# Moving an expert loop within its instruction blocks, clearing sums earlier, and splitting the first picks

## The chip, the cores and the metric

The kernel runs on one core of a Trainium2 chip. The metric is the time of one execution on the device in microseconds; three executions of the kernel before gave 1177.3, 1177.52 and 1179.76, median 1177.52.

## The reference

The kernel computes three transformer layers on 256 tokens of width 1024, in fp32. The third (with its own normalisations, a recurrence, neighbourhood attention and gates) isn't touched here. Each of the first two ends in a mixture of experts:

```
g_prob = softmax(x @ w_group + b_group);  g_w, g_idx = top_k(g_prob, 1)     # one of 4 groups
e_logits = (x @ w_router + b_router)[g_idx]                                 # 4 experts in it
e_val, e_idx = top_k(e_logits, 2);  e_w = softmax(e_val)
gates = sum(one_hot(4 * g_idx + e_idx, 16) * g_w * e_w)
for e in range(16):
    hid = silu(x @ w_gate[e]) * (x @ w_up[e])
    y = y + gates[:, e] * (hid @ w_down[e])
```

Each token thus uses 2 of 16 experts, and all weights of all 16 are read: 6 MB per expert.

## The kernel before, in words

**Weights.** All large weights come through a ring of six slots of 2 MB in SBUF. SP issues one transfer per slot (L437 in the expert layers, L417 elsewhere), in the order of use, as soon as PE has reported that it is done with the slot's previous content (`unit_done`).

**Routing.** PE computes router logits; VectorE picks group and experts and writes a mask of tokens by experts. PE turns the mask into ranks by five small matmuls (L790 to L794): the rank of each token within its expert. VectorE makes of them a key per token and expert (L2203), and of the key the "picks" of a pair of experts: for 128 columns, which token stands in which (L2223 and L2226). Beside this, PE has the two gate rows (L593), copied out by ScalarE (L1437), and the matmuls of a group of the next modulation vector (`group_main`, L550) to do.

**The loop.** 16 experts go as 8 pairs, in a loop on each engine. For each pair PE multiplies the gathered tokens (128 columns in four chunks of 32) by the gate and up weights of the two experts, gathers the next pair's tokens (L826), turns `hid` (L908), scatters the previous pair's results by adding them to four banks of sums (L891), turns the weighted picks (L916), and multiplies by the down weights. The four banks of sums are cleared before the loop by four bf16 matmuls of zeros (`clear_sums`, L811). How many of the four chunks go to the first expert of the pair depends on the tokens: 2 is the usual split, 1 and 3 are uneven. Each of the three has its own copy of the code, so that there are three bodies for gate and up (64 matmuls of the program each, L870) and three for down (32 each), chosen by branches (`by_split`, L853 and L857). With "usual first" the usual body stands ahead of the others, and leaves by a branch over them; with "usual last" it stands behind them, and is entered by a branch. `ahead` and `later` are hints that tell the sequencer of a branch to come. A token that finds no place in its expert's columns goes through code for left-over tokens, which stands behind the loop and is branched over when there is none (L971).

**Where the code lies.** `pe.addr_align(256, 101, 0)` (L787) asks that the next instruction be loaded at slot 101 of a block of 256 instructions; the loader branches over what it leaves empty. It stands right ahead of the mask matmuls, in each of the two layers, so all bodies of the loop lie at fixed slots of their blocks.

**Order.** The order on each engine is written out by hand, as the code is; nothing is scheduled. Semaphores order the engines against each other.

Of the kernel before, what the change touches and what calls it, by code (L numbers as in the profile page):

```python
# [21 lines left out]
ALU = mybir.AluOpType  # L22
# [110 lines left out]
def program(nc, a, out):  # L133
    ctx = ExitStack()
    with ctx:
# [151 lines left out]
        def copied_at(group):  # L287

            return group + 1
# [171 lines left out]
        def _(pe):  # L461
# [93 lines left out]
            def group_whole(group, last):  # L555

                pe.wait_ge(sem("ada_ready"), 4 * group)
                pe.wait_ge(sem("modulation_summed"), summed_at(unit_of[f"ada{last}"]))
                part = sum_of(last)
                for g in range(4):  # L560
                    mm = pe.matmul(group_bank(group)[32 * g:32 * g + 32, :], ones[:, 0:32],
                                   part[:, 512 * g:512 * g + 512], start=True, stop=True, tile_position=(0, 32 * g))
                mm.then_inc(sem(f"group_{group}_whole"), 1)
# [200 lines left out]
            def experts(layer):  # L764
# [11 lines left out]
                mm.then_inc(sem("logit_parts_full"), 1)  # L776
                gate_row(gate, 0)
                pe.wait_ge(sem("constants_ready"), 2 * layer + 2)
                pe.wait_ge(sem("logit_parts_taken"), layer + 1)
                for t in range(TT):  # L780
                    mm = pe.matmul(ps[4][:, S + 20 * t:S + 20 * t + 20], logit_parts[:, t * P:(t + 1) * P], sel,
                                   start=True, stop=True)
                mm.then_inc(sem("logits_full"), 1)
                gate_row(gate, 1)
                group_main(group, (2,))

                pe.addr_align(256, 101, 0)  # L787
                pe.wait_ge(sem("mask_ready"), 2 * layer + 2)
                mask = rt[:, 512:512 + 32].rearrange("p (t e) -> p t e", e=EXPERTS)
                pe.matmul(ps[4][:, 384:400], lt, mask[:, 0, :], start=True, stop=True)  # L790
                pe.matmul(ps[4][:, 400:416], ones, mask[:, 0, :], start=True, stop=False)
                pe.matmul(ps[4][:, 400:416], lt, mask[:, 1, :], start=False, stop=True)
                pe.matmul(ps[4][:, 416:432], ones, mask[:, 0, :], start=True, stop=False)
                pe.matmul(ps[4][:, 416:432], ones, mask[:, 1, :], start=False, stop=True)\  # L794
                  .then_inc(sem("rank_full"), 1)
                group_main(group, (3,))

                def left_over():

                    pe.wait_ge(sem("ada_part_taken"), copied_at(group))  # L800
                    pe.wait_ge(sem("over_ready"), layer + 1)
# [3 lines left out]
                def clear_sums():  # L805

                    taken(pe, gate)
                    pe.wait_ge(sem("constants_ready"), 2 * layer + 3)
                    zero = hidT[:, 0:2, :].rearrange("p a b -> p (a b)").bitcast(BF16)
                    for b in range(4):  # L810
                        mm = pe.matmul(ps[b][:, :], zero[:, 0:P], zero, start=True, stop=True, skip_group_check=True)  # L811

# [126 lines left out]
                clear_sums()  # L939
# [4 lines left out]
                with pe.Fori(0, PAIRS) as j:  # L944

                    which = pe.snap(split_reg)
                    pe.reg_alu(uneven_reg, split_reg, 1, ALU.bitwise_and)
                    ahead = pe.mark_branch_hint_location(uneven_reg)
                    later = []
                    by_split("gate_up", which, lambda n: gate_up(j, n), "usual first", ahead)  # L950
                    with pe.If(j > 0):
                        results(j - 1)
                    with pe.If(j < PAIRS - 1):
                        gather(j + 1)
                    turn_hid(j)
                    with pe.If(j > 0):
                        scatter(j - 1)
                    turn_weights(j)
                    by_split("down", which, lambda n: down(j, n), "usual last", first_uneven=later[0])
                    pe.wait_ge(sem("g_cur_ready"), j + (done + 1))  # L960
# [278 lines left out]
        def _(act):  # L1239
# [109 lines left out]
            def group_copy(group):  # L1349
                if group in SUMMED_GROUPS:  # L1350
                    act.wait_ge(sem(f"group_{group}_whole"), 1)
# [382 lines left out]
        def _(dve):  # L1734
# [345 lines left out]
            def route(layer):  # L2080

                lg = rt[:, 0:40].rearrange("p (t c) -> p t c", c=20)
                dve.wait_ge(sem("logit_parts_full"), layer + 1)
                dve.tensor_copy(logit_parts, ps[4][:, 0:S]).then_inc(sem("logit_parts_taken"), 1)
                dve.wait_ge(sem("logits_full"), layer + 1)
# [50 lines left out]
                for t in range(TT):  # L2136
# [3 lines left out]
                       .then_inc(sem("mask_ready"), 1)  # L2140
# [34 lines left out]
                dve.wait_ge(sem("rank_full"), layer + 1)  # L2175
# [25 lines left out]
                dve.tensor_tensor(by_tile(over), by_tile(rank), slots_bc, ALU.is_gt).then_inc(sem("over_ready"), 1)  # L2201
# [3 lines left out]
                dve.wait_ge(sem("over_ready"), layer + 1)  # L2205
                return weights

            def experts(layer):
# [12 lines left out]
                def picks(j):  # L2221
# [5 lines left out]
                       .then_inc(sem("pick_ready"), 1)  # L2227

# [42 lines left out]
                picks(0)  # L2271
# [611 lines left out]
```

## Time and profile before

| | us |
|---|---|
| three executions | 1177.3, 1177.52, 1179.76 |
| the profiled execution | 1178.81 |
| its span | 1177.1 |
| PE busy | 1114.5 (95%) |
| VectorE busy | 414.2 (35%) |
| ScalarE busy | 272.4 (23%) |

PE is busy nearly all the time. The two expert loops run from 183.6 to 410 and from 576.3 to 810 us. Rows marked PE are matmuls, PEld weight loads; an fp32 matmul of the program shows as two of each. A timeline row merges neighbouring instructions of one kind: start, length, engine, line, count (x), and in brackets how long the engine had been idle and what ended that. "issue" means that the profile shows nothing the engine waited for. q1 is the queue that carries the weights, q8 the one with PE's instructions.

### The profile page before, as it was taken

The page shows a single profiled execution, that of the slowest core. Times are in us where ns is not written, and L with a number is a line of the kernel's source. Part 1 is how long each engine was busy: PE and PEld are TensorE (multiplying, and loading weights), DVE is VectorE, ACT ScalarE, POOL GpSimd, SP SyncE. Part 2 cuts the span into 40 slices and gives each one's busy share as a digit, 9 for nine tenths or more (in the row PEclk, how much of TensorE's full clock was granted, in tenths as well). Part 3 has the DMA queues.
Part 4 walks back from the last instruction along what each step waited for, and adds up shares of the span by engine and source line. Part 5 has one row for each costly group of instructions (what it writes and reads, how often), then busy time and mean ns, then how long its engine had stood idle before and what let it go on. Part 6 is the DMA issues. An engine that isn't in the chain of part 4 may idle for free.

```text
span 1177.1 us, 17038 instructions
## 1 busy us (share of the span) xinstructions
PE 1114.5 (95%) x6890; PEld 646.3 (55%) x6891; DVE 414.2 (35%) x1065; ACT 272.4 (23%) x579; POOL 91.5 (8%) x156
## 2 busy tenths in 40 slices
PE   3999989999999999989899999998999999999997
PEld 0756434444444378554344444444886878767883
DVE  0275254112111089943511111114541444341213
ACT  2214332111111031162211111114002555541201
POOL 0300030000000000230000000000010323210000
PEclk9999999999999999999899999998999999999999
DMA  9998899999999987995799999999595455344000
GB/s 363 365 355 344 213 417 376 424 425 429 428 428 428 411 325 297 293 274 181 317 379 425 428 429 429 429 430 387 174 291 176 150 167 174 104 149 155 18 1 36
DMA packets 69380, 353.83 MB, mean 301 GB/s; under 512 B 5540, under 2 KB 7756, under 8 KB 49868
## 3 DMA queue, kind: packets, MB, share of 16 engines
q1 hardware_dynamic: 61656, 340.68, 75.1%
q0 software_dynamic: 6000, 9.17, 2.9%
q10 hardware_dynamic: 1668, 3.21, 0.7%
q8 instruction: 38, 0.62, 0.2%
q14 instruction: 18, 0.15, 0.0%
HBM read 350.84 MB, written 1.15 MB: 299 GB/s over the span
## 4 chain that ended last, share of the span: by engine, by line
PE 77%; DMA 15%; DVE 4%; ACT 2%; issue 2%; ACTq 0%; SPq 0%; DVEq 0%
PE bank L497 29%; PE bank L870 22%; DMA ring<-in_moe_w_up 11%; PE bank L535 8%; PE bank L826 3%; PE bank L891 3%; DMA arena<-in_ev_w_s 2%; DVE arena L1738 2%; DMA ring<-in_ev_w_in 2%; PE bank L550 1%; PE bank L1145 1%; PE bank L521 1%; PE bank L509 1%; PE bank L711 1%; PE bank L726 1%
## 5 line engine op out<-in xcount | busy, mean ns | idle before, releaser
L870 PE MATMUL bank<-ring,arena 128*32 128x512 f32 x3072 | 337.5, 595 | 9.7 <-issue 3.9
L497 PE MATMUL bank<-arena,ring 128*128 128x256 f32 x1536 | 340.0, 382 | 1.9 <-ACT arena L1286 1.7
L497 PEld LDWEIGHTS bank<-arena,ring 128*128 128x128 f32 x1536 | 290.5, 191 | 47.3 <-issue 8.7
L870 PEld LDWEIGHTS bank<-ring,arena 128*32 128x32 f32 x3072 | 102.3, 110 | 231.5 <-issue 229.7
L535 PE MATMUL bank<-ring,arena 128*128 128x512 f32 x288 | 126.0, 593 | 0.0
L535 PEld LDWEIGHTS bank<-ring,arena 128*128 128x128 f32 x288 | 54.2, 190 | 65.2 <-issue 64.8
L2258 DVE TENSOR_TENSOR arena<-arena,bank 128x512 f32<-128x512 f32 x16 | 11.0, 687 | 197.0 <-PE bank L870 197.0
L826 PEld LDWEIGHTS bank<-arena 128*128 128x128 f32 x512 | 58.5, 192 | 12.0 <-issue 11.7
L826 PE MATMUL bank<-arena 128*128 128x128 f32 x512 | 61.2, 278 | 0.0
L1464 ACT ACTIVATE arena<-bank 128x512 f32<-128x512 f32 x16 | 9.6, 597 | 210.5 <-PE bank L870 210.5
L891 PE MATMUL bank<-arena 128*128 128x512 f32 x128 | 57.7, 594 | 0.0
L1738 DVE SCALAR_TENSOR_TENSOR arena<-arena,cv 128x256 f32<-128x256 f32 x144 | 57.6, 480 | 0.1
L1360 ACT ACTIVATE arena<-bank 128x512 f32<-128x512 f32 x41 | 23.6, 595 | 142.0 <-PE bank L497 110.5
L1456 ACT ACTIVATE arena<-bank,mod,gs 128x128 f32<-128x128 f32 x64 | 24.1, 458 | 122.2 <-PE bank L826 122.2
L1738 DVE SCALAR_TENSOR_TENSOR arena<-arena 128x256 f32<-128x256 f32 (+4 forms) x57 | 21.2, 404 | 67.6 <-ACT arena L1659 63.8
L550 PE MATMUL bank<-ring,c_rep 128*32 128x512 f32 x320 | 43.7, 684 | 1.1 <-ACT c_rep L1253 0.8
L1738 DVE SCALAR_TENSOR_TENSOR arena<-ring,c_rep,arena 128x2048 f32<-128x2048 f32 (+1 forms) x21 | 38.2, 1818 | 6.7 <-DMA ring<-in_w_ada 5.8
L1290 ACT ACTIVATE arena<-x 128x512 f32<-128x512 f32 x20 | 12.5, 626 | 107.6 <-DVE x L1962 91.1
L2244 DVE TENSOR_SCALAR arena<-bank,gs,mod 128x128 f32<-128x128 f32 x64 | 21.9, 405 | 42.9 <-PE bank L826 42.8
L891 PEld LDWEIGHTS bank<-arena 128*128 128x128 f32 x128 | 23.2, 191 | 23.0 <-issue 23.0
L2811 POOL DMA_DIRECT2D arena<-arena x16 | 8.6, 561 | 328.2 <-DVE arena L1738 328.2
L1741 DVE CUSTOM_DVE_ANT_1 arena<-bank,arena 128x256 f32<-128x256 f32 x32 | 12.3, 422 | 62.0 <-PE bank L711 54.3
(327 smaller groups left out, 900.6 us busy)
## 6 DMA issues: line engine op xcount, KB each, us to landing
ring<-in_moe_w_gate SPq DMA_DIRECT2D x32, 2048.0 KB, 14.7
ring<-in_moe_w_up SPq DMA_DIRECT2D x32, 2048.0 KB, 17.2
ring<-in_moe_w_down SPq DMA_DIRECT2D x32, 2048.0 KB, 13.0
ring<-in_w_ada SPq DMA_DIRECT2D x24, 2048.0 KB, 21.7
ring<-in_w_in SPq DMA_DIRECT2D x16, 2048.0 KB, 11.2
ring<-in_w_c SPq DMA_DIRECT2D x6, 2048.0 KB, 32.8
ring<-in_ev_w_in SPq DMA_DIRECT2D x5, 2048.0 KB, 14.5
ring<-in_od_w_in SPq DMA_DIRECT2D x5, 2048.0 KB, 15.5
```

Of the source, the lines that this page charges most:

```text
L497: mm = pe.matmul(ps[k0][:, t * S:(t + 1) * S], w[:, k, c:c + P], rhs[:, k, :], start=(k == 0), stop=(k == KT - 1))
L535: mm = pe.matmul(ps[k0][:, :], lhs[:, k, b * P:(b + 1) * P], w[:, k, :], start=(i == 0), stop=(i == KT - 1))
L550: mm = pe.matmul(bank[32 * g:32 * g + 32, :], c_rep[:, side, k, :], w[:, k % 2, 512 * g:512 * g + 512], start=(k == 0), stop=(k == KT - 1) ...
L826: mm = pe.matmul(ps[6 + b][:, (k % 4) * P:(k % 4 + 1) * P], xn[:, t, k * P:(k + 1) * P], pick[:, t, :], start=(t == 0), stop=(t == TT - 1))
L870: mm = pe.matmul(bank[col:col + CHUNK, :], lhs[:, k, col:col + CHUNK], ring[:, (s0 + e) % RING, cut], start=start, stop=stop, tile_positio ...
L891: mm = pe.matmul(ps[2 * t + half][:, :], g_cur[:, t * P:(t + 1) * P], y_pair[:, half * 512:(half + 1) * 512], start=False, stop=True, skip ...
L1290: act.activation(half_of(squares, t, h), half_of(x, t, h), ACT.Square, scale=1.0 / 32, accum_out=sq(t, h))\
L1360: act.activation(dst, v, func, scale=scale).then_inc(free, 1)
L1456: ins = act.activation(x_cur[:, k, :], ps[6][:, k * P:(k + 1) * P], ACT.Identity, bias=mod[:, sh + k:sh + k + 1], scale=gs[:, 2 * layer + ...
L1738: return dve.scalar_tensor_tensor(out_, in0, scalar, in1, op0, op1)
L1741: return dve.tensor_tensor_reduce(out_, in0, in1, 1.0, start, op0, op1, acc)
L2244: ins = dve.tensor_scalar(x_cur[:, k, :], ps[7][:, (k - 4) * P:(k - 3) * P], gs[:, 2 * layer + 1, 0, k:k + 1], mod[:, sh + k:sh + k + 1], ...
```

## The change

Three edits go together, in both layers. (1) The alignment becomes slot 214, and the usual body of down goes first rather than last. (2) `clear_sums` is called behind the alignment and ahead of the wait for the mask. (3) The first pair's picks are made by `first_picks`: two compares and two fused compare-and-adds of 128x128, one for each tile of tokens, and behind them one compare of 128x256 for the weighted picks. Several semaphores are merged into `routing_sums_full`, `routed` and `group_whole`, with counts in place of names. PE waits for the first pick by `routed` and for the second by `pick_ready`.

```diff
-                mm.then_inc(sem(f"group_{group}_whole"), 1)
+                mm.then_inc(sem("group_whole"), 1)
...
-                pe.wait_ge(sem("logit_parts_taken"), layer + 1)
+                pe.wait_ge(sem("routed"), 5 * layer + 1)
...
-                pe.addr_align(256, 101, 0)
-                pe.wait_ge(sem("mask_ready"), 2 * layer + 2)
+                def clear_sums():
+
+                    taken(pe, gate)
+                    pe.wait_ge(sem("constants_ready"), 2 * layer + 3)
+                    zero = hidT[:, 0:2, :].rearrange("p a b -> p (a b)").bitcast(BF16)
+                    for b in range(4):
+                        mm = pe.matmul(ps[b][:, :], zero[:, 0:P], zero, start=True, stop=True, skip_group_check=True)
+
+                pe.addr_align(256, 214, 0)
+                clear_sums()
+                pe.wait_ge(sem("routed"), 5 * layer + 3)
...
-                  .then_inc(sem("rank_full"), 1)
+                  .then_inc(sem("routing_sums_full"), 1)
...
-                clear_sums()
+                pe.wait_ge(sem("routed"), 5 * layer + 5)
                 pe.wait_ge(sem("pick_ready"), done + 1)
                 pe.reg_load(split_reg, split[0:1, layer, 0:1])
...
-                    by_split("down", which, lambda n: down(j, n), "usual last", first_uneven=later[0])
+                    by_split("down", which, lambda n: down(j, n), "usual first")
...
+                def first_picks():
+
+                    iota = kc[:, K_IOTA:K_IOTA + P]
+                    for t in range(TT):
+                        step(dve.tensor_scalar(is_slot[:, t, 1, :], iota, key[:, t, 1:2], None, ALU.is_equal))
+                    step.wait()
+                    for t in range(TT):
+                        stt(pick[:, t, :], iota, key[:, t, 0:1], is_slot[:, t, 1, :], ALU.is_equal, ALU.add)\
+                            .then_inc(sem("pick_ready" if t else "routed"), 1)
+                    step_(dve.tensor_tensor(is_slot[:, :, 0, :], bc(key[:, :, 0:1], [P, TT, P]),
+                                            bc(iota.unsqueeze(1), [P, TT, P]), ALU.is_equal), 0, 1)
...
-                picks(0)
+                first_picks()
                 weights()
                 weighted_picks(0)
```

PE's order around the mask, before (L787 is the alignment, L790 to L794 the mask matmuls, L550 modulation, L811 the clearing, L826 the gather):

```order
L550 MATMUL bank<-ring,c_rep 32x512 x8
L787 ISA
L790 MATMUL bank<-arena,kc 128x16
L791 MATMUL bank<-arena,kc 128x16
L792 MATMUL bank<-arena,kc 128x16
L793 MATMUL bank<-arena,kc 128x16
L794 MATMUL bank<-arena,kc 128x16
L550 MATMUL bank<-ring,c_rep 32x512 x8
L811 MATMUL bank<-arena 128x512 x4
L941 TENSOR_LOAD split
L826 MATMUL bank<-arena 128x128 x16
```

The same place in the changed kernel (L795 is the alignment, L793 the clearing, L799 to L803 the mask matmuls, L942 the register load, L827 the gather):

```order
L550 MATMUL bank<-ring,c_rep 32x512 x8
L795 ISA
L793 MATMUL bank<-arena 128x512 x4
L799 MATMUL bank<-arena,kc 128x16
L800 MATMUL bank<-arena,kc 128x16
L801 MATMUL bank<-arena,kc 128x16
L802 MATMUL bank<-arena,kc 128x16
L803 MATMUL bank<-arena,kc 128x16
L550 MATMUL bank<-ring,c_rep 32x512 x8
L942 TENSOR_LOAD split
L827 MATMUL bank<-arena 128x128 x16
```

The clearing has moved from between the modulation matmuls and the register load to ahead of the mask matmuls; nothing else has moved here.

PE's down bodies before (L853 and L857 choose, L851 leaves an uneven body; the last L870 is the usual one):

```order
L853 COMPARE_AND_BRANCH
L857 COMPARE_AND_BRANCH
L870 MATMUL bank<-ring,arena 32x512 x32
L851 UNCONDITIONAL_BRANCH
L847 BRANCH_PREFETCH_HINT
L870 MATMUL bank<-ring,arena 32x512 x32
L851 UNCONDITIONAL_BRANCH
L870 MATMUL bank<-ring,arena 32x512 x32
```

And in the changed kernel (L854, L858 and L852 are those branches, L839 leaves the usual body, L871 are the matmuls):

```order
L854 COMPARE_AND_BRANCH
L871 MATMUL bank<-ring,arena 32x512 x32
L839 UNCONDITIONAL_BRANCH
L858 COMPARE_AND_BRANCH
L848 BRANCH_PREFETCH_HINT
L871 MATMUL bank<-ring,arena 32x512 x32
L852 UNCONDITIONAL_BRANCH
L848 BRANCH_PREFETCH_HINT
L871 MATMUL bank<-ring,arena 32x512 x32
L852 UNCONDITIONAL_BRANCH
```

The usual body now follows its compare and ends in a branch over the other two; the first uneven body has a hint of its own.

VectorE's picks in the changed kernel (L2204 makes the key; L2234, L1739 and L2239 are the new ones, in place of L2223 with 128x512 and L2226 with 128x256):

```order
L2204 TENSOR_TENSOR arena<-arena 128x32
L2234 TENSOR_SCALAR arena<-kc,arena 128x128 x2
L1739 SCALAR_TENSOR_TENSOR arena<-kc,arena 128x128 x2
L2239 TENSOR_TENSOR arena<-arena,kc 128x2x128
L2155 TENSOR_TENSOR arena<-arena 128x2
```

The weights of the pair (from L2155 on) stand behind them as they did before.

## Rows read from the trace of the kernel before

**Rows 1.** The page: its span, and the queue that carries PE's instructions.
```profile
span 1177.1 us, 17038 instructions
...
q8 instruction: 38, 0.62, 0.2%
```
**Rows 2.** PE timeline, first layer, body of the first pair and what follows.
```profile
183.57 13.94 PE L870 MATMUL bank<-ring,arena 128*32 128x512 f32 x128
197.44 3.84 PE L826 MATMUL bank<-arena 128*128 128x128 f32 x32
```
**Rows 3.** PE timeline, second layer, routing, first pair, last pair.
```profile
566.90 0.40 PE L790 MATMUL bank<-arena,kc 128*128 128x16 f32 x2 [1.91 <-DVE arena L2137]
...
571.60 1.04 PE L811 MATMUL bank<-arena 128*128 128x512 bf16 x4
572.48 3.73 PE L826 MATMUL bank<-arena 128*128 128x128 f32 x32
...
576.28 1.05 PE L870 MATMUL bank<-ring,arena 128*32 128x512 f32 x4
581.20 15.62 PE L870 MATMUL bank<-ring,arena 128*32 128x512 f32 x124 [3.86 <-issue]
596.75 3.84 PE L826 MATMUL bank<-arena 128*128 128x128 f32 x32
...
798.76 0.75 PE L908 MATMUL bank<-kc,arena 128*128 128x128 f32 x4 [0.80 <-DVE arena L2258]
```
**Rows 4.** PE weight loads (PEld) in the second layer, around the stop.
```profile
576.28 0.14 PEld L870 LDWEIGHTS bank<-ring,arena 128*32 128x32 f32 x5
581.20 0.15 PEld L870 LDWEIGHTS bank<-ring,arena 128*32 128x32 f32 x7 [4.77 <-issue]
```
**Rows 5.** A stretch: length, PE, PEld, DVE, ACT, POOL busy; granted clock; DMA share, GB/s.
```profile
581.20:584.93 3.73, 3.73 (x20) 1.23 (x23) 0.50 (x2) 0.00 (x0) 0.00 (x0) 0.54 0.11 44
```
**Rows 6.** DMA queues between 578.9 and 580 us: an instruction packet.
```profile
q8 instruction: 1, 0.02, 5.5%
```
**Rows 7.** The compare that chooses an uneven gate_up or down body: both in the second layer.
```profile
L857 PEldq COMPARE_BRANCH  x2: 68/68/69, 575.1 to 602.5; - x2
```
**Rows 8.** Waits of PE between 576 and 811 us: sum, times, longest.
```profile
PE bank L870 <- DMA ring<-in_moe_w_up: 1.9, 4, 0.5
```
**Rows 9.** DMA queue 1 between 650 and 819 us: packets, MB, share.
```profile
q1 hardware_dynamic: 8352, 71.47, 101.1%
```
**Rows 10.** All DMA between 582.83 and 591.1 us.
```profile
DMA packets 0, 0.00 MB, mean 0 GB/s; under 512 B 0, under 2 KB 0, under 8 KB 0
```
**Rows 11.** Timeline of SP's DMA issues before and in the second layer's first pair.
```profile
565.05 7.03 SPq L437 DMA_DIRECT2D ring<-in_moe_w_down  x2
590.15 0.94 SPq L437 DMA_DIRECT2D ring<-in_moe_w_gate  x2
```
**Rows 12.** DMA queue 1 between 200 and 320 us (first layer).
```profile
q1 hardware_dynamic: 3504, 51.12, 100.5%
```
**Rows 13.** ACT timeline, second layer: copies of the gate rows.
```profile
563.59 1.05 ACT L1437 COPY gate_bc<-bank 128x512 f32<-128x512 f32 x2
```
**Rows 14.** DVE timeline, second layer: the first pair's picks.
```profile
570.29 0.69 DVE L2223 TENSOR_TENSOR arena<-arena,kc 128x512 f32<-128x512 f32 x1
571.02 0.42 DVE L2226 TENSOR_TENSOR arena<-arena 128x256 f32<-128x256 f32 x1
```
**Rows 15.** Branch after a usual gate_up body: ns min/median/max, first and last start.
```profile
L838 PEldq COMPARE_BRANCH  x15: 189/189/328, 194.8 to 795.2; - x15
```
**Rows 16.** The branch behind the expert code, in both layers.
```profile
L971 PEldq COMPARE_BRANCH  x2: 329/336/342, 417.9 to 820.4; - x2
```
**Rows 17.** PE timeline behind that branch, first layer.
```profile
419.82 3.45 PE L497 MATMUL bank<-arena,ring 128*128 128x256 f32 x12
```
**Rows 18.** The same, second layer.
```profile
822.05 2.21 PE L497 MATMUL bank<-arena,ring 128*128 128x256 f32 x5
```
**Rows 19.** DMA queue q8 between 241 and 409 us.
```profile
q8 instruction: 1, 0.02, 0.0%
```

More of the change, by code:

```diff
@@ L775, in experts @@
                                        start=(r == 0), stop=(r == 1), tile_position=(0, 32 * g))
-                mm.then_inc(sem("logit_parts_full"), 1)
+                mm.then_inc(sem("routing_sums_full"), 1)
                 gate_row(gate, 0)
                 pe.wait_ge(sem("constants_ready"), 2 * layer + 2)
-                pe.wait_ge(sem("logit_parts_taken"), layer + 1)
+                pe.wait_ge(sem("routed"), 5 * layer + 1)
                 for t in range(TT):
@@ L782, in experts @@
                                    start=True, stop=True)
-                mm.then_inc(sem("logits_full"), 1)
+                mm.then_inc(sem("routing_sums_full"), 1)
                 gate_row(gate, 1)
                 group_main(group, (2,))
-                pe.addr_align(256, 101, 0)
-                pe.wait_ge(sem("mask_ready"), 2 * layer + 2)
+                def clear_sums():
[7 more added lines that the diff above has]
+                pe.wait_ge(sem("routed"), 5 * layer + 3)
                 mask = rt[:, 512:512 + 32].rearrange("p (t e) -> p t e", e=EXPERTS)
@@ L800, in left_over @@
                     pe.wait_ge(sem("ada_part_taken"), copied_at(group))
-                    pe.wait_ge(sem("over_ready"), layer + 1)
+                    pe.wait_ge(sem("routed"), 5 * layer + 4)
                     pe.matmul(ps[5][:, 480:512], ones, rt[:, 576:608], start=True, stop=True)\
                       .then_inc(sem("over_full"), 1)
[L805 to L811, printed above, removed]
                 def landed(m, j):
@@ L1350, in group_copy @@
                 if group in SUMMED_GROUPS:
-                    act.wait_ge(sem(f"group_{group}_whole"), 1)
+                    act.wait_ge(sem("group_whole"), SUMMED_GROUPS.index(group) + 1)
                 else:
@@ L2082, in route @@
                 lg = rt[:, 0:40].rearrange("p (t c) -> p t c", c=20)
-                dve.wait_ge(sem("logit_parts_full"), layer + 1)
-                dve.tensor_copy(logit_parts, ps[4][:, 0:S]).then_inc(sem("logit_parts_taken"), 1)
-                dve.wait_ge(sem("logits_full"), layer + 1)
+                dve.wait_ge(sem("routing_sums_full"), 3 * layer + 1)
+                dve.tensor_copy(logit_parts, ps[4][:, 0:S]).then_inc(sem("routed"), 1)
+                dve.wait_ge(sem("routing_sums_full"), 3 * layer + 2)
                 dve.wait_ge(sem("rw_loaded"), 16 * 7 * (layer + 1))
@@ L2139, in route @@
                                       bc(both[:, t, :].unsqueeze(1), [P, 4, 4]), ALU.mult)\
-                       .then_inc(sem("mask_ready"), 1)
+                       .then_inc(sem("routed"), 1)
                 dve.wait_ge(sem("route_exp_ready"), 2 * layer + 2)
@@ L2174, in route @@
                 few, other_many, lean = (rt[:, 708 + 8 * n:716 + 8 * n] for n in range(3))
-                dve.wait_ge(sem("rank_full"), layer + 1)
+                dve.wait_ge(sem("routing_sums_full"), 3 * layer + 3)
                 step(dve.tensor_copy(number, ps[4][:, 416:432]))
@@ L2200, in route @@
                 step(dve.tensor_tensor(by_tile(within), by_tile(rank), slots_bc, ALU.is_le))
-                dve.tensor_tensor(by_tile(over), by_tile(rank), slots_bc, ALU.is_gt).then_inc(sem("over_ready"), 1)
+                dve.tensor_tensor(by_tile(over), by_tile(rank), slots_bc, ALU.is_gt).then_inc(sem("routed"), 1)
                 step.wait()
@@ L2204, in route @@
                 step.wait()
-                dve.wait_ge(sem("over_ready"), layer + 1)
+                dve.wait_ge(sem("routed"), 5 * layer + 4)
                 return weights
```

## The prediction

> **What bounds the kernel now.** I read the page first: a span of 1177.1 us [rows 1]. The profiled execution took 1178.81 us, 1.7 more than its span and 1.3 more than the median of 1177.52. All sums are made against this execution. Then came PE's timeline through both expert layers, because the change touches nothing else, then the clock by stretches, the DMA between the same moments, and last the waits.
>
> The two layers run the same code on different tokens, so they should read alike. They don't. In the first layer the body of the first pair runs from 183.57 to 197.44, 13.87 us [rows 2]. In the second it starts at 576.28, does four matmul rows, stands still for 3.86 us with "issue" as the releaser, and reaches the gather only at 596.75: 20.47 us [rows 3]. That is 6.6 us more for the same 128 rows. The weight loads show 4.77 us without one [rows 4]. Right behind the stop the granted clock is 0.54 for 3.73 us, between the two levels of 1.2 and 2.4 GHz and nearly all of it at the lower, after an engine that had done nothing [rows 5]. So of the 6.6 us about 4.8 is the stop and 1.8 the clock after it.
>
> What does the stop stand for? A packet of 16 KB goes through the instruction queue between 578.9 and 580 us [rows 6], inside the stop. PE had entered the uneven code at 575.1, by the compare that stands there [rows 7], and the branch to it is 0.4 us earlier, 574.7. The 38 packets of that queue carry 0.62 MB [rows 1], 16 KB each; the call in the kernel aligns to 256 slots, so a packet is one block of 256 instructions. One fp32 matmul of the program is two weight loads and two matmul rows, four slots. Counting from slot 101, where the kernel pins the mask matmuls: 61 slots to the load of `split`, then 70 to the loop's set-up, head at slot 233, the usual body from 237 on. The uneven bodies follow 261 slots later, and the body for "1" has its first weight load at slot 248 of the next block. Eight instructions fit before the edge; four matmul rows [rows 3] and five loads [rows 4] are what it did. That compare ran twice, both times in the second layer [rows 7]: its first pair takes this uneven body, every other pair the usual one. The stop is a jump that lands just short of a block's edge, before the block behind it has been fetched.
>
> The second question is who sets the end of a layer. Four waits on `in_moe_w_up` in the second layer sum to 1.9 us [rows 8] and 0.80 more comes at the last pair [rows 3], while queue 1 is at 101% from 650 to 819 [rows 9]. The transfers set the end. But they had stood still: no packet moved between 582.83 and 591.1 [rows 10], 8.27 us, because the ring was full and its next slot came free only at 590.15, when the first pair's gate half was done [rows 11]. In the first layer queue 1 is at 100.5% from 200 to 320 [rows 12].
>
> **The change part by part.**
> *Place of the loop.* Slot 214 in place of 101, and the clearing now behind it: 62 + 1 + 69 + 1 slots put the head at slot 91 of the next block. The uneven "1" body then has its first weight load near slot 106, 150 slots before the edge, 75 load-and-matmul pairs. At 13.94 us for 128 [rows 2], 0.109 us each, that is 8.2 us. From the branch at 574.7 to the first work behind the edge at 581.20 [rows 3] it took 6.5 us, so the block should be there in time. Gain on PE: 6.6 us, stop and clock together. The bounds are 0 (the stop stays) and 6.6.
>
> *Clearing in the wait.* The four bf16 matmuls occupy PE from 571.60 to 572.48, 0.88 us, behind the last modulation matmuls [rows 3]. Ahead of the mask PE idles 1.91 us [rows 3], and what the clearing waits for is done: the gate rows' copies end at 564.64 [rows 13], 0.35 us before PE falls idle at 564.99. So it hides fully, 0.9 us inside 1.9. Were this cover gone it would hold back the mask matmuls by at most 0.88. What is late next is the pick.
>
> *Four small picks.* Now 0.69 us for 128x512 and 0.42 us for 128x256, from 570.29 to 571.44 [rows 14]. 256 elements cost 0.27 more, so 128 take about 0.28; neighbours overlap by 0.09. Two compares and two fused ones: 0.47, a wait of about 0.04, 0.47, ready near 571.27, 0.15 us sooner. PE's register load of `split` stands behind this; it was hidden under the clearing and is now in the open. Before, first gather matmul 572.48 and pick at 571.44, with the clearing between them. After, 571.27 plus the load (0.3 to 0.5) and a hand-over of 0.1 to 0.3 gives 571.7 to 572.1. I take 572.0: a gain of 0.5 in each layer, bounds 0 and 0.9. The added 128x256 compare and the later weights (0.4 us) fall before VectorE's next wait for the gather, when it has 2.8 us idle; they cost nothing, at worst 0.4.
>
> *Down bodies, usual one first.* The usual body now runs on without a branch and leaves by one over two bodies of 128 slots. A branch costs the sequencer 0.19 us, 0.33 where it is first taken [rows 15], while PE works off what is queued. I take 0; at worst a first visit stalls PE by 0.5 us once a layer, which the later DMA waits absorb. *Semaphores:* three merged counters with the same order of events, 0.
>
> *What the ring makes of it.* In the second layer PE is 6.6 + 0.5 = 7.1 us ahead when the gate half is done: the slots come free at 583.05, not 590.15. The previous transfers drain at 582.83, so the gap shrinks from 8.27 to about 1.2 us, and the transfers, and with them the end of the layer, move by 7.1. PE alone would have moved by 7.1 plus the 2.7 us of waits; that surplus is lost, the waits grow. In the first layer queue 1 never stands still, so the 0.5 us mostly vanish; 0.2 to 0.4 may stay through a slot freed sooner. I take 0.3.
>
> Sum: 7.1 + 0.3 = 7.4 us. From the profiled 1178.81 that is 1171.4, from the median of 1177.52 it is 1170.1. I forecast 1170.8 between the two.
>
> **The rivals.**
> *A cold jump behind the loop (slower).* Past the experts PE branches over 366 slots of code for left-over tokens, at 417.9 and 820.4 [rows 16]. Before, it stands at slot 53 of a block and lands at slot 163 of the next one, and the work behind it starts at 419.82 and 822.05 [rows 17, 18] with no stall. In the new layout it stands at slot 168 and lands at slot 22 of the block after the next. No packet for that block is seen to be asked for from there. If it must be fetched, 6.5 us pass from the branch: work starts at 424.4 and 826.9, 4.6 and 4.8 us late, all of it on PE's path, since queue 1 no longer bounds there. 1170.8 + 9.4 = 1180.2, and up to 1.8 us more per layer for the clock. It decides if both layers pay more than 3.7 us. For it: the stop shows that a block not asked for in time costs several us, and nothing in the new code asks for the far one. Against it: in the steady loop PE branches over two whole bodies in 0.19 us [rows 15] with a single instruction packet in 168 us [rows 19], so blocks once fetched are kept, and what else is fetched ahead the trace leaves open.
> The Trainium skill, "Runtime: NRT & Kernel Launch", section "Instruction fetch mechanics", says that prefetch is sequential and that a taken branch whose target isn't in the current window of two pages forces a fetch before execution goes on. By that rule this rival comes true in both layers. The trace agrees with the sequential part at the stop of the second layer, but not with a window of two: the loop's own jump goes two blocks on and costs 0.19 us. I give it less than half for that.
>
> *The stop only moves.* The jump to the uneven body now needs its own block, asked for when PE passes into the one before, about when the mask arrives (566.90 [rows 3]) or up to 1.4 us later; 6.5 us on is 573.4 to 574.8, the jump comes at 574.2. If it is late, or the hint's block goes first, up to 4 us come back: 1174.8.
>
> *The stop has another cause.* Then only 0.5 us per layer is left on PE, and the second layer's reaches the ring: 1178.1, no change to be seen.
>
> **How the numbers follow.** Forecast as worked out 55%, cold jump 22%, stop moved 15%, other cause 8%. Its own range is 1167.8 to 1173.5: the pick term at 0 to 0.9 in both layers, a gap refilled a little better or worse, and the 1.3 us between profiled run and median. A measurement of this kernel tells about 0.2%, 2.4 us. Faster by more: 55% and most of the moved stop, 68%. Within it: the other cause, the milder cold jumps and a moved stop that takes all, 14%. Slower: 18%. The range for 8 in 10 takes in the moved stop and the other cause and leaves most of the cold jump out: 1167.5 to 1179.
>
> **What would show it.** In the new profile: the second layer's first body 13.9 us long with no wait on "issue" and a clock of 1.00; the four clearing matmuls between 565 and 566; gather at about 572.0 less what the first layer gave; the slots freed near 583 and queue 1 idle for about 1 us there; more than four waits on `in_moe_w_up`. Wrong would be a stretch of 4 us without a matmul behind the branch past the experts, or behind the edge of any body, or a layer whose end doesn't follow its transfers.

## The result, and the profile of the changed kernel

Over nine runs of each, the changed kernel takes 1185.57 us and the kernel before 1177.26 us. The ratio is 1.0064 with a 95% interval of 1.0038 to 1.009: it is slower by 0.6%. The forecast was 1170.8 us, faster. It was wrong in its sign. The likeliest case needed a warm jump behind the experts, one whose target is already loaded; the jump was cold, its target still had to be fetched. So one of the rivals, the cold jump, came true in both layers, and another, the stop that only moves, came true beside it.

The profiled execution took 1183.76 us with a span of 1182.1, against 1178.81 and 1177.1 [rows 1]: 5.0 us more in the span. I tell where they are in the order of time. (Lines of the changed kernel are mostly one number higher: gate, up and down are L871, the gather is L827, the branch past the left-over code is L972.)

The branch behind the expert code, answering to [rows 16]. The columns are instruction, count, ns (least/median/most) and first and last start:
```profile
L972 PEldq COMPARE_BRANCH  x2: 5993/6074/6156, 417.1 to 820.0; - x2
```
It took 336 ns before; now both visits take 6 us. PE's timeline around it, first and second layer, answering to [rows 17, 18]:
```profile
409.20 1.06 PE L572 MATMUL bank<-kc,arena 128*128 128x4 f32 x8
...
416.94 1.07 PE L610 MATMUL bank<-kc,arena 128*128 128x128 f32 x8 [0.40 <-ACT arena L1322]
423.28 1.19 PE L497 MATMUL bank<-arena,ring 128*128 128x256 f32 x2 [5.28 <-issue]
...
819.79 1.94 PE L610 MATMUL bank<-kc,arena 128*128 128x128 f32 x8 [0.60 <-ACT arena L1322]
826.28 2.05 PE L497 MATMUL bank<-arena,ring 128*128 128x256 f32 x4 [4.55 <-issue]
```
Work behind the branch begins at 423.28 and 826.28, 3.46 and 4.23 us later than before, although the code ahead of it had been 0.8 and 0.4 us early (L572 stood at 410.01 before). So the jump costs 4.3 and 4.6 us; the rest of its 6 us lies under work that was already queued, and under a short wait that the kernel before has there too. The queues between the branch and the work behind it, second layer:
```profile
q1 hardware_dynamic: 1179, 2.38, 103.7%
q8 instruction: 1, 0.02, 1.0%
```
There is one packet on PE's instruction queue (q8), at 823.56, 3.6 us behind the branch (first layer: 420.6, 3.5 us behind). Nothing on that queue goes ahead of it for 200 us. And the clock, from the stop on and behind it:
```profile
820.00:826.20 6.20, 1.73 (x8) 1.33 (x7) 5.04 (x13) 2.68 (x8) 0.00 (x0) 0.50 1.05 385
826.28:829.62 3.34, 3.34 (x8) 2.71 (x9) 3.20 (x5) 0.00 (x0) 0.00 (x0) 0.50 1.05 384
```
The seventh field behind the window is the granted clock: 0.50 is 1.2 of the 2.4 GHz. In the second layer it is at 0.50 already for the eight matmuls ahead of the stop, as it was in the kernel before; what is new is that it stays there for 3.3 us after work has come back. In the first layer it is 1.00 ahead of the stop (416.90 to 418.10) and 0.50 for 3.57 us behind it.

The second layer, answering to [rows 3]:
```profile
568.04 0.81 PE L793 MATMUL bank<-arena 128*128 128x512 bf16 x3 [0.16 <-issue]
569.79 0.40 PE L799 MATMUL bank<-arena,kc 128*128 128x16 f32 x2 [0.94 <-DVE arena L2138]
...
571.01 1.92 PE L550 MATMUL bank<-ring,c_rep 128*32 128x512 f32 x16
574.68 3.81 PE L827 MATMUL bank<-arena 128*128 128x128 f32 x32 [1.74 <-DVE arena L1739]
578.32 0.31 PE L811 MATMUL bank<-arena,kc 128*128 128x32 f32 x2
581.17 13.94 PE L871 MATMUL bank<-ring,arena 128*32 128x512 f32 x128 [2.54 <-issue]
595.05 3.84 PE L827 MATMUL bank<-arena 128*128 128x128 f32 x32
...
601.37 20.97 PE L871 MATMUL bank<-ring,arena 128*32 128x512 f32 x192 [1.80 <-issue]
622.27 3.84 PE L827 MATMUL bank<-arena 128*128 128x128 f32 x32
...
673.00 7.07 PE L871 MATMUL bank<-ring,arena 128*32 128x512 f32 x64 [0.25 <-DMA ring<-in_moe_w_up]
...
798.34 0.75 PE L909 MATMUL bank<-kc,arena 128*128 128x128 f32 x4 [0.80 <-DVE arena L2271]
```
The mask matmuls come at 569.79, 2.89 us later than before: that is what is left of the first layer's jump. Count from there. The gather at 574.68 is 0.7 us earlier than 572.48 + 2.89. The first body has 128 rows in 13.94 us with no break, but it stands 2.54 us on "issue" ahead of its first row, and the next gather at 595.05 is 4.6 us earlier than 596.75 + 2.89 in place of the 7.1 forecast. At the last pair 3.3 are left (798.34 against 798.76 + 2.89).

The branch into the uneven body shows what the 2.54 us are:
```profile
L854 PEldq COMPARE_BRANCH  x32: 66/79/3582, 181.1 to 800.5; - x32
```
The longest of 32, at 577.0, took 3.58 us, and an instruction packet goes at 578.22.

From 4.6 us at the second gather to 3.3 at the last pair another 1.3 us go. The first down body takes 0.6 of them: from 595.05 to the next gather at 622.27 are 27.22 us, where the kernel before had 26.63. The wait ahead of that body is 1.80 us, and was this:
```profile
602.64 20.81 PE L870 MATMUL bank<-ring,arena 128*32 128x512 f32 x192 [1.36 <-DVE arena L2244]
```
This pair takes an uneven body, and with the usual one first the way to it is a taken branch (425 ns at 600.67, 78 ns at 602.38 before). The other 0.7 is seen in the transfers. The pause was 8.27 us [rows 10]; now it is 3.65, from 585.77 to 589.42. But the four slots that come free at 588.5 and 595.2 are filled in some 19.6 us, 8.4 MB at 428 GB/s, and the next come free at 608.5, so the queue runs thin a second time:
```profile
600.00:610.00 10.00, 8.63 (x80) 2.79 (x84) 3.46 (x7) 0.26 (x1) 0.00 (x0) 1.00 1.00 421
610.00:620.00 10.00, 10.00 (x97) 3.63 (x93) 0.25 (x1) 0.60 (x1) 0.00 (x0) 1.00 0.96 370
```
The last field is GB/s; the kernel before moved 424 in that second stretch.

So the 5.0 us of the span are: +3.5 from the first layer (its 0.8 gained and 4.3 lost), -0.6 up to the second mask, -3.3 in the second layer, +4.6 at its end and +0.8 in the tail, where the lower clock lasts 3.34 us behind the branch against 1.81 before. The medians differ by 8.3 us. The profiled run here is 1.8 below the median of its kernel, and the one before was 1.6 above its own, which makes up the rest.

### The profile page after: what moved, and what is told of

Same layout as the page of the kernel before. It is cut to its first block, busy times and chain, and to the rows that moved or that the text cites. A ratio compares the mean times of both kernels' runs of the same rounds, so it can differ in the third digit from the quotient of the medians.

```text
span 1182.1 us, 17059 instructions
## 1 busy us (share of the span) xinstructions
PE 1108.6 (94%) x6888; PEld 646.2 (55%) x6891; DVE 414.4 (35%) x1071; ACT 272.1 (23%) x579; POOL 91.4 (8%) x156
## 3 DMA queue, kind: packets, MB, share of 16 engines
HBM read 350.84 MB, written 1.15 MB: 298 GB/s over the span
## 4 chain that ended last, share of the span: by engine, by line
PE 74%; DMA 16%; DVE 4%; ACT 3%; issue 2%; ACTq 0%; SPq 0%; DVEq 0%
PE bank L497 29%; PE bank L871 20%; DMA ring<-in_moe_w_up 13%; PE bank L535 8%; PE bank L827 3%; PE bank L892 2%; DMA arena<-in_ev_w_s 2%; DVE arena L1739 2%; DMA ring<-in_ev_w_in 1%; PE bank L521 1%; PE bank L509 1%; PE bank L1146 1%; PE bank L550 1%; PE bank L711 1%; PE bank L726 1%
## 5 line engine op out<-in xcount | busy, mean ns | idle before, releaser
L497 PE MATMUL bank<-arena,ring 128*128 128x256 f32 x1536 | 343.6, 384 | 11.5 <-issue 9.8
L871 PE MATMUL bank<-ring,arena 128*32 128x512 f32 x3072 | 335.1, 593 | 9.4 <-issue 4.8
L871 PEld LDWEIGHTS bank<-ring,arena 128*32 128x32 f32 x3072 | 102.1, 110 | 229.1 <-issue 227.6
L827 PEld LDWEIGHTS bank<-arena 128*128 128x128 f32 x512 | 58.4, 192 | 17.2 <-issue 11.7
L827 PE MATMUL bank<-arena 128*128 128x128 f32 x512 | 61.4, 278 | 3.7 <-DVE arena L1739 3.7
L1739 DVE SCALAR_TENSOR_TENSOR arena<-arena,cv 128x256 f32<-128x256 f32 x144 | 57.6, 479 | 0.1
L1739 DVE SCALAR_TENSOR_TENSOR arena<-arena 128x256 f32<-128x256 f32 (+4 forms) x57 | 21.1, 404 | 73.9 <-ACT arena L1660 63.8
L550 PE MATMUL bank<-ring,c_rep 128*32 128x512 f32 x320 | 40.1, 635 | 1.1 <-ACT c_rep L1254 0.8
L1739 DVE SCALAR_TENSOR_TENSOR arena<-ring,c_rep,arena 128x2048 f32<-128x2048 f32 (+1 forms) x21 | 38.2, 1818 | 7.0 <-DMA ring<-in_w_ada 6.1
```

The costliest lines, as they stand in the source:

```text
L497: mm = pe.matmul(ps[k0][:, t * S:(t + 1) * S], w[:, k, c:c + P], rhs[:, k, :], start=(k == 0), stop=(k == KT - 1))
L550: mm = pe.matmul(bank[32 * g:32 * g + 32, :], c_rep[:, side, k, :], w[:, k % 2, 512 * g:512 * g + 512], start=(k == 0), stop=(k == KT - 1) ...
L827: mm = pe.matmul(ps[6 + b][:, (k % 4) * P:(k % 4 + 1) * P], xn[:, t, k * P:(k + 1) * P], pick[:, t, :], start=(t == 0), stop=(t == TT - 1))
L871: mm = pe.matmul(bank[col:col + CHUNK, :], lhs[:, k, col:col + CHUNK], ring[:, (s0 + e) % RING, cut], start=start, stop=stop, tile_positio ...
L1739: return dve.scalar_tensor_tensor(out_, in0, scalar, in1, op0, op1)
```

## The experiments

The theory: **(T)** a block of 256 instructions is asked for when PE's sequencer (the part that reads the instructions and queues them, ahead of the work itself) enters the block before it, or when a jump finds it missing, and is there some 6 us later; the loss is the jump past the left-over code, whose target fell into the block after the next. The rival: **(R)** clearing in the wait, small picks, merged counters or the order of the down bodies cost the time. Two smaller rivals stand with their runs. Runs e1 to e4 go with a median of 1177.74 us for the kernel before, e5 to e8 with 1178.03.

**e1_place: the kernel before, only moved.**
```
-                pe.addr_align(256, 101, 0)
+                pe.addr_align(256, 215, 0)
```


> The kernel before with one number changed: the code is pinned at slot 215 in place of 101, which puts the loop's head at slot 91 as in the changed kernel; clearing, picks, semaphores and the order of the down bodies stay as before. Theory (the place alone is the loss, by a cold jump behind each loop): the branch past the experts takes about 6 us in both layers (0.34 us before), PE stands still 4 to 5 us behind each, the stop in the second layer's first pair shrinks from 3.9 to about 2.5 us and moves ahead of the body; median about 1186, as slow as the changed kernel or a little slower, since the gather's 0.5 us per layer isn't gained. Rival (the new order of clearing, picks or counters costs the time, not the place): the branch stays at 0.3 us and the median within 2 us of 1177.3.


Measured: 1191.56 us, ratio 1.0112 (1.0089 to 1.0134). The place alone makes the kernel slower, and by more than the whole change does, so R isn't needed for the loss; whether its parts cost anything is for e7 to tell. The branch takes 6108 and 6184 ns. My number was 5.6 us short, and the timeline of the first layer shows by what:
```profile
204.78 1.92 PE L870 MATMUL bank<-ring,arena 128*32 128x512 f32 x15 [1.58 <-DVE arena L2244]
211.53 21.90 PE L870 MATMUL bank<-ring,arena 128*32 128x512 f32 x177 [4.84 <-issue]
```
The first down body stops after 15 rows, for 4.84 us. With the usual body last, this place lays its start just ahead of an edge, in the block that PE has jumped to a moment before. The changed kernel has the usual body first and stops there for 0.45 us:
```profile
209.87 13.94 PE L871 MATMUL bank<-ring,arena 128*32 128x512 f32 x128 [0.45 <-issue]
```

**e2_back: the changed kernel at the old place.**
```
-                pe.addr_align(256, 214, 0)
+                pe.addr_align(256, 100, 0)
```


> The changed kernel with one number changed: pinned at slot 100 in place of 214, so that the loop's head is at slot 233 again as in the kernel before; clearing ahead of the mask, small picks, merged counters and the usual down body first all stay. Theory (place is the loss): the branch past the experts takes 0.3 us again, the 3.9 us stop in the second layer's first pair is back, both layers gain 0.5 us ahead of the gather of which the second passes on 0.5 and the first 0.3; median about 1176.5, that is 0 to 1.5 below the kernel before. Rival (clearing, picks or counters cost the time): 1183 or more with the branch at 0.3 us.


Measured: 1181.34 us, 1.0032 (1.0018 to 1.0046). The branch past the left-over code takes 0.34 us again. But the time is neither T's 1176.5 nor R's 1183. A third jump is cold, the one that leaves the usual down body over the two uneven ones:
```profile
L839 PEldq COMPARE_BRANCH  x30: 169/184/5858, 194.2 to 809.2; - x30
```
PE's timeline around it, first layer:
```profile
202.60 7.08 PE L871 MATMUL bank<-ring,arena 128*32 128x512 f32 x64 [1.23 <-DVE arena L2257]
213.95 15.64 PE L871 MATMUL bank<-ring,arena 128*32 128x512 f32 x128 [4.28 <-issue]
```
The branch of 5858 ns is at 206.93, a packet follows at 210.25, and PE stands for 4.28 us; the body behind needs 15.64 us in place of 13.94, 1.7 more, by the clock. By slots the target is number 240 of the next block. That it was missing says that it, or something that goes with it, lay behind the edge; the run doesn't show which.

**e7_back_last: the same with the old order of the down bodies.**
```
-                    by_split("down", which, lambda n: down(j, n), "usual first")
+                    by_split("down", which, lambda n: down(j, n), "usual last", first_uneven=later[0])
```


> The kernel e2 (changed kernel at the old place) with the usual down body last again. It is the kernel before with only the clearing ahead of the mask, the small picks and the merged counters. Theory (e2 lost to a cold branch of 5.9 us that leaves the usual down body in the first layer, which the old order of the bodies doesn't have): no branch over 0.4 us but the stop of the second layer's first pair, 4.3 us less in the first layer than e2; median 1176.5 to 1177.5, the kernel before less the 0.3 to 0.8 us of the picks. Rival (clearing, picks or counters cost the 3.6 us): 1181.


Measured: 1175.61 us, 0.9974 (0.9959 to 0.9988). It gains 5.7 us on e2 by the medians, 6.8 by the ratios: 4.3 of stop and 1.7 of clock make 6.0. This kernel is the one before with clearing, picks and counters changed, and it is 2.4 us below it, more than the 0.3 to 0.8 that I gave them. These parts don't cost time, and R falls. The time is 0.9 us below the range that I gave. Whether all of the 2.4 is theirs is open: the interval reaches from 1.4 to 4.8 us.

The four combinations together. Place old and usual body last: 1175.6. Old, first: 1181.3. New, first: 1185.6 (the change). New, last: 1191.6 (with the old picks). The order that costs 5.7 us at one place saves time at the other. How much isn't told cleanly: the difference is 6.0, but it holds clearing, picks and counters too, which together may be worth 1.4 to 4.8 (e7). The traces give 4.84 us of stop with the usual body last and 0.45 with it first.

**e3_hint: the changed kernel with a prefetch hint for the exit.**
```
+                past_late.append(pe.mark_branch_hint_location())
                 group_columns(group)
...
-                pe.br_cond(pe.snap(split_reg) > 0, f"late_pe{layer}", f"on_pe{layer}")
+                pe.br_cond(...).branch_hint(past_late[layer])
```


> The changed kernel plus one instruction behind each expert loop: a prefetch hint for the branch past the left-over code, about 8 us ahead of that branch. Nothing moves by more than a slot. Theory (the branch is long because its target's block was never asked for): an instruction packet shows near 413 and 815, the branch takes 0.3 us, 4.2 us (first layer) and 4.6 us (second) come back and with them about 1.5 us of low clock, median 1175 to 1177.5. Rival (the branch itself or the wait for the registers is slow in this layout, or the work behind it is late for another reason): the hint changes nothing, 1185.5. A third: the hint is dropped by the sequencer and no packet is seen; then 1185.5 too, and the packets tell these apart.


Measured: 1184.54 us, 1.0052 (1.003 to 1.0074), against before; the interval takes in the changed kernel's 1.0064. The hint stands at 409.4 and 810.4, 10.3 and 12.6 us ahead of its branch.
```profile
L975 PEldq COMPARE_BRANCH  x2: 5818/5912/6005, 419.6 to 823.1; - x2
```
No packet goes between 213.75 and 422.94 us, and that one is 3.3 us behind the branch at 419.6. So this is the third case of the expectation: the hint stands in the program and fetches nothing. It says nothing against T, and nothing for it. Why it fetched nothing is open.

**e4_exit_align: the exit entered early and brought next to its target.**
```
+                pe.addr_align(256, 0, 0)
                 group_columns(group)
                 results(PAIRS - 1)
```


> The changed kernel with the code behind each loop pinned at slot 0 of the next block: the branch past the left-over code then stands at slot 67 and lands at slot 177 of the block right behind, and that block is asked for when the code behind the loop begins, 8 us before the branch. Theory (a target in the block after the next is cold, one in the next block is warm if entered early enough): an instruction packet near 413 and 815, branch of 0.3 us, about 0.2 us for the extra branch in each layer, median 1175.5 to 1178. Rival (the distance does not matter): 1185.5.


Measured: 1174.50 us, 0.9976 (0.9962 to 0.999): 11.1 us below the changed kernel by the medians (10.4 by the ratios) and 3.2 below the kernel before.
```profile
L973 PEldq COMPARE_BRANCH  x2: 336/336/336, 419.1 to 817.5; - x2
```
Packets now go at 412.39 and 808.80, 3.4 and 3.9 us behind the branches at 408.9 and 804.9 that enter this code. The expected gain was 8 to 10 us: 8.9 are the two stops, and about 2 more is clock. The run is 1 us better than its range. In the second layer something else moved as well. The stop at the first body is 1.06 us in place of 2.54, but another has come in ahead of it, six matmul rows into the modulation group behind the mask:
```profile
568.26 1.06 PE L550 MATMUL bank<-ring,c_rep 128*32 128x512 f32 x6
570.39 3.52 PE L550 MATMUL bank<-ring,c_rep 128*32 128x512 f32 x10 [1.08 <-issue]
```
That is where, with the pin at 214, the block's edge lies by the count of slots.

**e6_far: the same, but two blocks from its target.**
```
-                pe.addr_align(256, 0, 0)
+                pe.addr_align(256, 90, 0)
```


> The kernel e4 with the code behind each loop pinned at slot 90 in place of 0 of the same block. Work, order, number of branches and the way to the branch stay; only the target of the branch past the left-over code falls into the block after the next (slot 11) in place of the next one (slot 177). Theory (a jump two blocks on is cold): that branch takes about 6 us in both layers in place of 0.34, a packet follows it by 3.3 us, and the time is that of e4 plus 4.3 and 4.6 us and some low clock: median 1183.5 to 1186. Rival (what e4 gained came from entering the code earlier or from the extra branch, not from the distance): 1174.5.


Measured: 1187.55 us, 1.0062 (1.0039 to 1.0085); that is 13 us above e4 by the medians and 10 by the ratios.
```profile
L973 PEldq COMPARE_BRANCH  x2: 6014/6143/6272, 419.2 to 826.0; - x2
```
```profile
425.38 43.69 PE L497 MATMUL bank<-arena,ring 128*128 128x256 f32 x192 [4.52 <-issue]
...
832.47 7.85 PE L497 MATMUL bank<-arena,ring 128*128 128x256 f32 x28 [4.71 <-issue]
```
The branch starts within 0.1 us of e4's in the first layer, behind the same work and the same extra branch. Branch and target both stand 90 slots further, and that puts the target over one more edge. 0.34 us becomes 6.0. That settles the distance for this branch, which has no hint. Stops of 4.5 and 4.7 us make 9.2 of it; the rest is clock (43.69 us for the 192 matmuls that e4 does in 41.68, so 2.0 there) and the second layer, whose stop at the first body came out at 3.68 in place of 1.06. The median is 1.6 us above the range that I gave.

**e5_early and e8_early2: the uneven bodies asked for earlier too.**
```
-                pe.addr_align(256, 214, 0)
+                pe.addr_align(256, 4, 0)        # e5; 244 in e8
...
+                pe.addr_align(256, 0, 0)        # ahead of group_columns, as in e4
```


> The kernel e4 (changed kernel, code behind each loop pinned at slot 0 of the next block) with the mask matmuls and the clearing pinned at slot 4 in place of 214. The block that holds the uneven bodies is then asked for when PE enters the pinned code, before the wait for the mask, and the edge inside the uneven body lies 105 slots behind its start. Theory (a block is there about 6.5 us after the sequencer enters the one before): no wait on issue at the first pair's body in either layer, branch to the uneven body 0.3 us, first body 13.9 us, the transfers' pause in the second layer 1 to 2 us; against e4, which stopped 1.1 us at the body's start and 1.1 before the last group of modulation matmuls, 2 to 2.5 us less: median 1172 to 1172.5. Rival (the uneven body's stop has its own cause, the first use of that code): 1174.5 as e4.


Measured: 1171.31 us, 0.9931 (0.9908 to 0.9955), the fastest kernel of the study. Its second layer, answering to [rows 3] once more:
```profile
566.37 0.40 PE L799 MATMUL bank<-arena,kc 128*128 128x16 f32 x2 [0.93 <-DVE arena L2139]
...
571.24 3.81 PE L827 MATMUL bank<-arena 128*128 128x128 f32 x32 [1.73 <-DVE arena L1740]
574.89 0.31 PE L811 MATMUL bank<-arena,kc 128*128 128x32 f32 x2
575.12 13.94 PE L871 MATMUL bank<-ring,arena 128*32 128x512 f32 x128
589.00 3.84 PE L827 MATMUL bank<-arena 128*128 128x128 f32 x32
```
```profile
L854 PEldq COMPARE_BRANCH  x32: 66/79/329, 181.5 to 794.2; - x32
```
No wait on issue is left at these bodies: the longest of the 32 branches is 329 ns, where the changed kernel had 3582. From mask to second gather it takes 22.63 us, against 29.85 before: 7.2 less, where the forecast had 7.1. The transfers pause for 0.84 us in place of 8.27 (the forecast: 1.2). The rival, a stop that belongs to the first use of that code wherever it lies, is out. The median is 0.7 us below my range.

> As e5, pinned at slot 244: the next block is entered two instructions behind the clearing, at the wait for the mask, and the edge inside the uneven body lies 121 slots behind its start in place of 105. Theory: as e5, 1172 to 1172.5, the same within 0.5 us, with more room at the edge and less at the jump. Rival: as e4, 1174.5.


Measured: 1172.22 us, 0.9935 (0.9911 to 0.9959), the same as e5 within what the runs tell apart. So the order of the three places is T's: with the pin at 4 or 244 the block is asked for ahead of the mask (1171.3, 1172.2), at 214 behind it (1174.5).

The size at slot 214 is not T's. The edge there lies six rows into the modulation group, as e4's stop showed. In the changed kernel PE goes over it at 571.0, and the packet with the uneven bodies goes at 578.22, 7.2 us later; in e3 it is 7.2 too, in e6 8.3 and in e4 5.6. In e5 and e8 it goes 4.2 and at most 4.3 us behind the edge's crossing, and behind the branches above 3.3 to 3.9. What holds the request back at slot 214 is open.

Nor does T say why one far jump is warm on its first visit. The branch that leaves a usual gate and up body goes over two bodies of 256 slots each, so two blocks on or more, and the first time PE comes there it takes this, in the kernel before:
```profile
L838 PEldq COMPARE_BRANCH  x1: 328/328/328, 194.8 to 194.8; - x1
```
In the changed kernel it takes 430 ns. This branch has a prefetch hint at the head of the loop:
```profile
L948 PEldq BRANCH_PREFETCH_HINT  x1: 53/53/53, 181.9 to 181.9; - x1
```
The exit branch has none, nor has the branch in e2 that took 5.86 us. One packet goes between hint and branch (187.43); which block it brought isn't shown. The hint is the obvious reason, but no run took it out, and the one that e3 put in did nothing.

## Why the prediction was wrong, step by step

*What bounds the kernel, and the stop's cause.* Right. The stop in the second layer's first pair is a missing block: it moves when the code moves, and is gone in e5, where the block is asked for earlier.

*Place of the loop, "gain on PE: 6.6 us".* This is the step that failed, and for what it left out. It followed the one jump that had been seen to stall and asked whether that would be warm. The same move shifts every other jump and every edge against the blocks, and the sum had no term for any of them. Of these the jump past the left-over code fell from "next block" to "the block after": 4.3 and 4.6 us of stop, by e4 and e6 some 10 to 13 us with the clock. The cold jump was named as a rival, with 6.5 us from the branch to the work (measured 6.2 and 6.3), 4.6 and 4.8 us of stop (4.3 and 4.6), and 22% for it. The mechanism and its price were right and the weight was wrong. The argument that brought the weight down was that the loop's own branch goes over two bodies in 0.19 us [rows 15]. Nearly all of the fifteen in that row are jumps to blocks that PE had visited in an earlier turn. The longest, 328 ns at 194.8, is a first visit, and it was warm too; but that branch has a hint 12.9 us ahead of it, and the exit branch has none. The exit was put beside a branch that differs from it in two ways, an earlier visit and a hint.

The Trainium skill, "Runtime: NRT & Kernel Launch", "Instruction fetch mechanics", says that a taken branch out of the current two pages forces a fetch. For first visits without a hint e4 and e6 agree (0.34 us to the next block, 6.1 to the one after). For blocks already visited the trace doesn't agree: 0.19 us [rows 15]. Nor does it for the first visit with a hint, 0.33 us.

*The same step, the size of the 6.6.* The uneven body had its 150 slots to the edge and ran through. What went missing was the block in which it begins: the forecast had it there 6.5 us behind the edge, and it took 9.5, from 571.0 to 580.6. That is the rival "the stop only moves", put at 15% and up to 4 us; it took 2.5 us of stop at the body and with the queue behind it 3.8 of the second layer's 7.1. The forecast gave separate chances to two rivals that have one cause and don't exclude each other: both come from blocks asked for late. Together they are the result: from the profiled run 1171.4 + 3.8 + 8.9 = 1184.1, against 1183.76. That it comes so near is in part luck, for the 0.8 us of low clock in the tail aren't in the sum. The median, 1185.57, is not explained beyond this; a profile shows one run.

*Clearing in the wait.* Right: the clearing matmuls run at 568.04, the wait for the mask shrinks from 1.91 to 0.94 us, and nothing comes later for it. It does more than the forecast says. PE now waits less ahead of the mask, and the modulation matmuls behind it take 1.92 us at a clock of 1.00 (571.00 to 572.95); before, they were these, at 0.55:
```profile
568.29 3.38 PE L550 MATMUL bank<-ring,c_rep 128*32 128x512 f32 x16
```
It doesn't come out so in every run: in e8, with the same clearing, they take 3.52.

*Four small picks.* Forecast 0.5 us per layer at the gather, found 0.7 in the second, but not by the picks:
```profile
573.02 0.48 DVE L2234 TENSOR_SCALAR arena<-kc,arena 128x128 f32<-128x128 f32 x2
573.54 0.61 DVE L1739 SCALAR_TENSOR_TENSOR arena<-kc,arena 128x128 f32<-128x128 f32 x2
```
From 573.02 to 574.15 are 1.13 us, against 1.15 before [rows 14]: the two fused ones take 0.61, not 0.47. PE waits for both tiles' picks ahead of its register load, so the split into tiles gives it nothing. What it gains is 0.5 us from the clearing, which no longer stands between pick and gather (0.53 us from one to the other, 1.04 before), and 0.16 from ranks that are there sooner (VectorE takes them up 1.40 us behind the start of the mask matmuls, 1.56 before). In the first layer the gather comes 0.9 us earlier, of which 0.4 came in from ahead of the mask; 0.8 are left at the end. So 0.4 of 0.5 stayed, where the forecast had 0.3.

*Down bodies, 0 and at worst 0.5.* At the new place 0.45 us in the first layer and 0.6 in the second, near the bound. But the bound was no bound: e2 shows 4.3 us for the same edit at the old place, and e1 shows 4.8 without it at the new one. The row that it rested on [rows 15] was again of later visits and of a branch with a hint.

*What the ring makes of it.* The mechanism is right: the pause shrinks by what PE gains (8.27 to 3.65 here, to 0.84 in e5). That a pause partly closed leaves the queue thin some 20 us later was not in it, about 0.7 us.

*The forecast as such* is met by a kernel that has both causes removed, at another place: 1171.31 us measured in e5, 1170.8 said. That is no merit of the forecast, which was made for slot 214.

## What to carry to other kernels

Where code is longer than what the sequencer has asked for ahead, list every jump and every block edge in the path of each first visit before moving anything, and ask of each: which block, when was the block before it entered, and does the branch have a hint that is seen to work? A place is only good or bad for all of them at once. When one mechanism explains a stop that you remove, look for the same mechanism in what you create, and don't take the speed of a loop's tenth turn as evidence on its first, or that of a hinted branch as evidence on one without a hint.

## What the runs showed of the hardware

A jump to a block not yet asked for costs the sequencer 5.8 to 6.3 us: nine such branches in the changed kernel, e1, e2, e3 and e6 are between 5818 and 6272 ns. The packet goes 3.3 to 3.7 us behind the branch. Some 1.5 us of the cost hides under work already queued. A target in the next block costs 0.33 to 0.44 us if the block of the branch was entered 10 to 13 us earlier (e4, e5, e8). A first visit two blocks on or more cost 0.33 us where a hint stood 12.9 us ahead (kernel before).

Behind the stop PE works at 1.2 GHz for a while (a granted clock of 0.50 for the first 3.6 us in e6 and in the changed kernel's first layer): 1.7 us more for a body of 128 rows (e2), 2.0 for 192 projection matmuls (e6).

A prefetch hint placed 10.3 and 12.6 us ahead of a compare branch sent no packet at all (e3). A plain branch into the block before the target brought it in time, for 0.3 us (e4).
